# Eight expert bodies on TensorE: where the next width is looked up, and when scattered rows are added

## The reference, cut to what matters

```python
def moe_swiglu(h, w_router, wg, wu, wd):
    logits = einsum('td,de->te', t, w_router)
    top_logit, top_e = lax.top_k(logits, 2)
    gates = softmax(top_logit)
    ...                                   # tokens gathered by expert
    (silu(xb @ wg[e]) * (xb @ wu[e])) @ wd[e]      # D_FF = 2816
    y = zeros_like(t).at[tok_sorted].add(out[dest] * gate_sorted[:, None])
xp = xp + mp[5] * fp        # the gate row multiplies the sum of the experts
```

## Time and profile before

| | us |
|---|---|
| median of 3 runs | 2300.97 (2299.86 to 2304.49) |
| the profiled execution | 2302.15 |
| its span, from first to last instruction | 2300.3 |
| PE busy (matmuls), share | 2103.9, 91% |
| DVE busy, share | 506.0, 22% |
| ACT busy, share | 394.5, 17% |
| mean granted TensorE clock | 0.947 |

### The profile page before, as it was taken

One profiled execution on the slowest core, in us unless ns is written; L12 is line 12 of the kernel. 1 busy time (PEld: TensorE's weight loads), 2 busy tenths in 40 slices (PEclk: granted clock), 3 DMA queues, 4 the chain that ended last, 5 costly groups with the idle time before them and its releaser, 6 DMA issues.

```text
span 2300.3 us, 28109 instructions
## 1 busy us (share of the span) xinstructions
PE 2103.9 (91%) x12187; PEld 1368.0 (59%) x12187; DVE 506.0 (22%) x1148; ACT 394.5 (17%) x843; POOL 49.1 (2%) x26
## 2 busy tenths in 40 slices
PE   4999978899999999879879999989999999997967
PEld 2554548785555687545864537667444784674543
DVE  2530145220000001364320102121211110212222
ACT  2221211210000002433111102112020110120311
POOL 0000024000000000000000000000000000000000
PEclk8999988999999999988969999999999799998989
DMA  9545320134454522110605565969687365595997
GB/s 334 184 146 178 115 92 1 37 110 134 159 188 159 181 76 90 59 45 1 212 8 183 183 200 202 337 214 340 214 298 251 112 222 200 182 343 164 389 336 304
DMA packets 221780, 412.93 MB, mean 180 GB/s; under 512 B 8655, under 2 KB 79790, under 8 KB 221358
## 3 DMA queue, kind: packets, MB, share of 16 engines
q1 hardware_dynamic: 218526, 409.35, 51.5%
q10 hardware_dynamic: 3088, 1.06, 0.2%
HBM read 407.59 MB, written 2.79 MB: 178 GB/s over the span
## 4 chain that ended last, share of the span: by engine, by line
PE 71%; DVE 5%; issue 3%; DMA 2%; ACT 1%; POOLq 0%; POOL 0%; ACTq 0%; DVEq 0%
PE bank L905 22%; PE bank L998 12%; PE bank L651 10%; PE bank L472 7%; PE bank L669 5%; PE bank L929 2%; DMA arena<-in_moe_w_down_dram 2%; PE bank L876 2%; PE bank L1021 1%; PE bank L410 1%; DVE arena L1825 1%; PE bank L442 1%; DVE X L1828 1%; PE bank L865 1%; PE bank L741 1%
## 5 line engine op out<-in xcount | busy, mean ns | idle before, releaser
L905 PE MATMUL bank<-ring,HTXN 128*32 128x128 f32 (+3 forms) x4352 | 411.8, 400 | 1.3 <-issue 1.3
L905 PEld LDWEIGHTS bank<-ring,HTXN 128*32 128x32 f32 (+2 forms) x4352 | 297.2, 123 | 105.0 <-issue 71.6
L1086 ACT ACTIVATE arena<-bank 128x512 f32<-128x512 f32 (+3 forms) x352 | 161.7, 527 | 755.7 <-PE bank L998 242.0
L998 PE MATMUL bank<-ring,arena 128*64 128x512 f32 (+2 forms) x640 | 228.9, 599 | 13.2 <-DVE arena L1816 9.3
L651 PE MATMUL bank<-HTXN,ring 128*128 128x384 f32 x704 | 231.7, 490 | 2.7 <-DVE HTXN L1424 2.7
L472 PE MATMUL bank<-ring,HTXN 128*128 128x512 f32 (+4 forms) x624 | 197.1, 478 | 3.7 <-DVE HTXN L1424 2.7
L651 PEld LDWEIGHTS bank<-HTXN,ring 128*128 128x128 f32 x704 | 133.7, 191 | 94.7 <-issue 5.5
L1812 DVE TENSOR_TENSOR arena<-arena,bank 128x512 f32<-128x512 f32 x120 | 76.2, 683 | 446.0 <-PE bank L905 446.0
L998 PEld LDWEIGHTS bank<-ring,arena 128*64 128x64 f32 (+2 forms) x640 | 80.8, 158 | 150.1 <-issue 141.8
L472 PEld LDWEIGHTS bank<-ring,HTXN 128*128 128x128 f32 x624 | 115.0, 192 | 81.8 <-issue 71.8
L1363 ACT ACTIVATE arena<-bank 128x512 f32<-128x512 f32 x120 | 64.1, 597 | 373.6 <-PE bank L905 373.6
(11 more groups left out here) (215 smaller groups left out, 1711.3 us busy)
## 6 DMA issues: line engine op xcount, KB each, us to landing
ring<-in_moe_w_gate_dram SPq DMA_DIRECT2D x64, 1024.0 KB, 6.1
ring<-in_moe_w_up_dram SPq DMA_DIRECT2D x64, 1024.0 KB, 5.4
ring<-in_moe_w_down_dram SPq DMA_DIRECT2D x64, 1024.0 KB, 7.4
ring<-in_w_mod_dram SPq DMA_DIRECT2D x24, 2048.0 KB, 12.2
arena<-in_moe_w_gate_dram SPq DMA_DIRECT2D x24, 1024.0 KB, 5.4
arena<-in_moe_w_up_dram SPq DMA_DIRECT2D x24, 1024.0 KB, 6.6
arena<-in_moe_w_down_dram SPq DMA_DIRECT2D x24, 1024.0 KB, 7.3
ring<-in_w_in_dram SPq DMA_DIRECT2D x10, 2048.0 KB, 8.7
```

Of the source, the lines that this page charges most:

```text
L905: last = mm(bank[row:row + rows_, col:col + cn], slots_of(k, i, at, rows_), wt[:, c0:c0 + cn], start=(k == 0 and col == 0), stop=(k == KT ...
L998: last = mm(out, act_of(f, i, w), wt[:, f % 2, 512 * h:512 * h + 512], start=(f == 0), stop=(f == FT - 1))
L1086: return act_fn(out, in_, ACT.Copy)
```

## The change

The `If`s are replaced by named blocks. The eight values are loaded once, ahead of expert 0. Each body ends with up to seven comparisons against the next expert's value, in the order 2, 1, 0, 3, 4, 5, 6, 7, each with its own jump to the start of that expert's body; expert 7's bodies jump to the end. The wait for gaA stands at the head of every body. VectorE multiplies all six scatter banks first, into the six places of `sgm`, and adds them later; the last expert does this in pairs. `upd` goes. ScalarE waits for the former expert's sums before its first SiLU of an expert.

```diff
-                this = pe.value_load(vtab[0:1, e:e + 1], min_val=0, max_val=len(WIDTHS) - 1)
-                with pe.If(this < 3):
...
+            ORDER = [2, 1, 0, 3, 4, 5, 6, 7]
+            pe.br("experts")
+            entry = nc.switch_body("experts", valid_engines=[mybir.EngineType.PE])
+            variant = [pe.value_load(vtab[0:1, e:e + 1], min_val=0, max_val=len(WIDTHS) - 1) for e in range(NE)]
...
+            def go_to(e, at):
+
+                if e == NE:
+                    pe.br(body_of(e, 0))
+                    return
+                for n, v in enumerate(ORDER[:-1]):
+                    pe.br_eq(variant[e], v, on_true=body_of(e, v), on_false=f"{at}_not{n + 1}")
+                    nc.switch_body(f"{at}_not{n + 1}", valid_engines=[mybir.EngineType.PE])
+                pe.br(body_of(e, ORDER[-1]))
+
+            go_to(0, "experts")
             for e in range(NE):
...
+                for v in ORDER:
+                    nc.switch_body(body_of(e, v), parent=entry, valid_engines=[mybir.EngineType.PE])
+                    if e > 0:
+                        for q in range(2):
+                            pe.wait_ge(*moe_drained(("gaA", q), e - 1))
+                    expert(e, PIECES[v])
+                    go_to(e + 1, body_of(e, v))
...
+                if e > 0:
+                    act.wait_ge(x_updated, 3 * NT + 6 * e)
...
-                for n in range(6):
-                    t, half = n // 2, n % 2
...
+                groups = [range(6)] if e + 1 < NE else [range(2 * t, 2 * t + 2) for t in range(NT)]
+                for group in groups:
+                    for n in group:
+                        dve.wait_ge(*moe_filled(("sc", n), e))
+                        v.tensor_tensor(sgm[:, n // NPIECE, n % NPIECE, :], moe_bank_of(("sc", n))[:, :],
+                                        GB[:, 0 if n < 2 else 1, 512 * (n % 2):512 * (n % 2) + 512], ALU.mult).then_inc(moe_drained(("sc", n), e)[0], 1)
+                    for n in group:
+                        dve.wait_ge(*moe_drained(("sc", n), e))
+                        x = X[:, n // 2, 512 * (n % 2):512 * (n % 2) + 512]
+                        v.tensor_tensor(x, x, sgm[:, n // NPIECE, n % NPIECE, :], ALU.add).then_inc(x_updated, 1)
+                dve.wait_ge(x_updated, 3 * NT + 6 * (e + 1))
```

More of the change, by code:

```diff
@@ L184, in hybrid_trunk @@
         OT = HT
-        (act_a, sgm_a, yt_a, pg_a, pgT_a, ps_a, iota, upd_a) = lay(
-            [9216, 2 * NPIECE * 512, NPIECE * D, NT * TOK, NT * TOK, NT * TOK, TOK, 1024])
+        (act_a, sgm_a, yt_a, pg_a, pgT_a, ps_a, iota) = lay(
+            [9216, 2 * NPIECE * 512, NPIECE * D, NT * TOK, NT * TOK, NT * TOK, TOK])
         sgm = sgm_a.rearrange("p (b i n) -> p b i n", b=2, i=NPIECE)
-        upd = upd_a.rearrange("p (b n) -> p b n", b=2)
         H2 = XN
@@ L1044, in _ @@
                 pe.wait_ge(*drained(("ga0", q)))
-            for e in range(NE):
-                if e > 0:
-                    for q in range(2):
-                        pe.wait_ge(*moe_drained(("gaA", q), e - 1))
-                this = pe.value_load(vtab[0:1, e:e + 1], min_val=0, max_val=len(WIDTHS) - 1)
-                with pe.If(this < 3):
[L1051 to L1077, removed]
@@ new lines, in _, with body_of @@
+            ORDER = [2, 1, 0, 3, 4, 5, 6, 7]
+            pe.br("experts")
+            entry = nc.switch_body("experts", valid_engines=[mybir.EngineType.PE])
+            variant = [pe.value_load(vtab[0:1, e:e + 1], min_val=0, max_val=len(WIDTHS) - 1) for e in range(NE)]
+            def body_of(e, v):
+                return f"expert{e}_width{WIDTHS[v]}" if e < NE else "experts_done"
+            def go_to(e, at):
[6 more added lines that the diff above has]
+                pe.br(body_of(e, ORDER[-1]))
@@ new lines, in _ @@
+            go_to(0, "experts")
+            for e in range(NE):
+                for v in ORDER:
[5 more added lines that the diff above has]
+                    go_to(e + 1, body_of(e, v))
+            nc.switch_body(body_of(NE, 0), parent=entry, valid_engines=[mybir.EngineType.PE])
```

## The result

The changed kernel takes 2237.34 us (median of 4 runs, 2236.11 to 2238.86) against 2300.85: ratio 0.9722, 95% interval 0.9704 to 0.9739. Single executions of one kernel differ more than I had assumed: 25 runs of before in one series lay between 2290.4 and 2308.5.

What follows compares the result with a forecast made beforehand. TensorE was taken as the bound, busy 91%, with 60.1 us of issue waits at the entry and between experts. Gains at boundaries, clock and weight stream, less 0.9 at the entry, summed to 46.7: 2254 us, range 2245 to 2272.

Steps and rivals of the forecast that it cites:

- Bound and mechanism: Expert boundaries: a race between sequencer (three far branches and a load, about 14 us), 6 us of scatter and VectorE's last multiply.
- The start 0.94 us after the scatter: Boundaries 1 to 2, 2 to 3, 3 to 4 and 5 to 6: new body starts 0.94 us after scatter's end.
- Experts 1, 2, 3 and 5: These experts with the boundary behind each: gains of 7.5, 4.8, 8.9 and 12.5 us.
- Experts 6 and 7: Last two experts, waiting for weights: the stream starts 15.7 us earlier and 8.2 us of pause goes.
- the pause: Weight stream from expert 6 to 7: its 8.2 us standstill goes if expert 7 releases in time.
- A miss: A comparison that doesn't jump: 0.08 us each; the rival that it costs like a far branch had chance 0.04.
- The added wait of ScalarE: Before an expert's first SiLU: hidden by some 0.8 us at least; if it shows, only expert 6 or 7 is touched.
- expert 0: Expert 0 with the boundary to expert 1: no gain, 0 us.
- the clock's term: Higher clock after shorter gaps: 1.9 us each at 1 to 2 and 2 to 3; 2.5 at 3 to 4, bounds 0 and 7.1.
- the clock holds: Rival: clock stays up through gather_more, 4.6 us more than forecast, 2248 with a cheap entry; chance, or more, 0.11.
- The entry: Ahead of expert 0: seven more loads 4.9 us, four comparisons 0.3, one far branch of 4.3 less; net cost 0.9.
- The tail: Kernel's end: the last expert's pairs keep the order of its three stores, 0 us, ends 0.5 either way.

Runs made afterwards that it cites:

- The two halves alone: New TensorE jumps with VectorE's old order: 2267.05 us; old TensorE program with VectorE's new order and ScalarE's new wait: 2299.29 us.
- delay_e4b: Changed kernel with 105 written waits ahead of expert 4's first matmul, making the gap there 3.96 us: 2251.13 us.
- before_moved128: Kernel before the change with 128 written (64 kept) early waits that move all later TensorE code by 64 instructions: 2295.41 us, ratio 0.9975.
- delay_e4: Changed kernel with 60 written waits (30 kept) ahead of expert 4's first matmul, gap there 1.82 us: 2245.38 us.
- load_at_exit: Changed kernel with the value loaded at each exit and the wait for gathered tokens moved from the entry into expert 0's bodies: 2237.71 us.
- warm_entry: load_at_exit with four extra matmuls of unused result queued ahead of the jump into expert 0: 2232.79 us, ratio to before 0.9708.
- stall_inside2: Changed kernel with 30 written waits inside turn_gates of expert 0, after its first piece: 2242.63 us.
- stall_inside3: The same kernel as stall_inside2, measured again, although its text speaks of 60 written waits: 2245.43 us.

## Why the prediction was wrong

Right, and shown:
- Bound and mechanism: each boundary is a race of sequencer, scatter and VectorE's last multiply. The start 0.94 us after the scatter measured 0.87. Experts 1, 2, 3 and 5 gave 32.2 us where the terms gave 33.7; 1.3 of the difference is the clock's fall at the start of expert 5, which some executions have and others don't. The two halves alone went as their expectations said.
- Experts 6 and 7: 11.4 us without the tail, against 11.5. The first load of expert 6 came 3.05 us after its body's start (3.25 forecast), and the pause is gone: where before the stream dried up, it runs on at 386 GB/s. The load, and a window over the change from expert 6 to 7:

```profile
2070.02 0.37 SPq L1946 DMA_DIRECT2D ring<-in_moe_w_up_dram  x1
```
```profile
2140.00:2160.00 20.00, 16.78 (x120) 11.79 (x120) 11.08 (x18) 3.81 (x8) 0.00 (x0) 0.83 1.05 386
```

- A miss takes 0.06 us, 0.13 with its distance to the next (0.08 forecast), and lies under the scatter. A far branch can be a little cheaper than the 3.6 us read from before's trace, whose shortest took 3.34. The added wait of ScalarE doesn't appear in ScalarE's list of waits.

Wrong. The profiled executions differ by 64.2 us where the sum had 46.7. Three terms make up the 17.5 that it lacks: expert 0 with 7.5, expert 4 with 6.3, and the stretch up to expert 0 with 3.9. The other rows come out at about nothing in sum.
- *"I take 2.5, nearer the low end, since work that didn't raise the clock in 8 us of being busy is more likely to let it fall."* This step of the clock's term failed. The 48 MATMULs of `gather_more`, which before ran at 0.50 throughout, kept a clock that was up, ten times of ten, and `delay_e4b` shows the loss when it is down. Expert 4 gained 8.8 us, even above the upper end of 7.1: 6.5 in `turn_gates` and `gather_more`, and 2.3 in the first gate chunks, which that end had left out. The rival "the clock holds" had the mechanism and too low a chance.
- The entry: *"Net cost 0.9"* was 0: 10.60 us from the last matmul to expert 0 against 10.61 before, the loads costing what the removed branch gave. What the sum lacked is expert 0 itself, 7.5 us. I had seen the 1.55 us stall there and used it only as a danger to the new kernel; that the old one pays it, and with it the slow clock, wasn't asked; the sum put expert 0 at nothing without a reason. `before_moved128` gives 5.4 us without the change. And part of the 7.5 comes and goes: in `delay_e4`, which has no stall but the low clock, expert 0 takes 215.97 us, so the stall's absence is worth 1.8 and the risen clock 5.7, and the clock rose in six of nine uninterrupted profiles of the new TensorE program. The prediction couldn't have known which it would get.
- The profiled execution's first 1188 us were taken as given. They varied by 3 us between executions of the same code, and that went into the first result as luck.
- The tail: 0 forecast, 1.3 measured. Pairs without a wait between them run 0.60 us apart, not 0.72.

The range was too narrow on the fast side because it took each clock effect as a loss that the change might bring, and none as a loss that it might end elsewhere.

## What to carry to other kernels

Where an engine has several bodies to choose from, let each end with its own comparisons for the next. In the changed kernel a miss took 0.13 us with its distance to the next and a far branch 3.3 to 4.3; under 5.3 us of queued scatter one far branch was hidden and three weren't. Then look for who is last next: the order in which the consumer frees the bank decided over a third of the gain. And price a gap on TensorE by what runs behind it: in the profiles, 3.35 us of idle cost 7.8 us of slow matmuls (expert 0 took 216.2 us in `load_at_exit` and 208.4 in `warm_entry`), and four matmuls put into it without use for their result paid for themselves.

Last, take one profile as one execution. The kernel of `stall_inside2` and `stall_inside3` had expert 0 fast in one and slow in the other, and an estimate to 3 us needs a median over several runs of both kernels.

## What the runs showed of the hardware

- In expert 4, 48 MATMULs of 64 columns, back to back for 10.5 us, ran at a granted clock of 0.50 throughout (`delay_e4b`); begun at 1.00, the same work took 5.6 us and kept it.
- The clock was also low (0.53 over 3 us) behind a gap of only 0.88 us, at the start of expert 5, in seven of eleven profiles.
- In the changed kernel a far branch took 3.3 to 4.3 us, and 6.3 at the last boundary, beside the weight stream at 386 GB/s (two profiles); a branch to the code right behind it took 0.18 us, a miss 0.06 to 0.08.
- Moving code by 64 instructions removed a stall of 1.5 us behind one landing, brought one of 1.8 us behind another, and changed the whole kernel by 5.4 us (1.4 to 10.1).
- The Trainium skill (Runtime: NRT & Kernel Launch, Instruction fetch mechanics) calls the crossing from one block of instructions to the next mostly hidden. The stall of 1.5 us behind a landing, which went with the move, wasn't hidden. Whether it is such a crossing no run here shows.
